# A transformer block on one core: attention scores on two row tiles and single-column sums on four column tiles

## The reference

```
mod = silu(c) @ ada_w + ada_b                  # 6 x 1024 shifts, scales and gates, one vector
h = rmsnorm(x, norm1_w) * (1 + scale1) + shift1
... = split(h @ w_in)                          # linear attention, 3 x 4 heads of dilated attention, merge gates
# dilated attention: group g of (window, dilation) = (128, 1), (512, 4), (2048, 16), 4 heads of width 64
s = einsum('brhnid,brhnjd->brhnij', q, k) / 8, masked to the band
m = max(s); p = exp(s - m); o = p @ v / sum(p)
o = sum over the groups, weighted by softmax(lse)
x = x + gate1 * (mixed @ w_out)
h2 = rmsnorm(x, norm2_w) * (1 + scale2) + shift2
x = x + gate2 * (ffn(h2) @ w_down)
return rmsnorm(x, final_norm_w)
```

## Time and profile before

| | |
|---|---|
| median of 3 runs | 909.78 us |
| the profiled execution | 910.8 us |
| its span | 909.0 us |
| granted clock over the span | 0.994 |
| TensorE busy | 890.8 us (98%) |
| VectorE, ScalarE busy | 494.3 us (54%), 368.8 us (41%) |
| TensorE waits, all: line 1780, first transfer | 7.0 us |
| line 2250 for ScalarE | 1.3 us |
| line 1817 and 1829 for VectorE | 1.0 and 0.4 us |
| line 1928 for ScalarE | 0.4 us |
| line 2282 for VectorE | 0.2 us |

### The profile page before, as it was taken

The page is one execution under the profiler, slowest core; times in us unless marked ns, Lnnn a source line. Parts: engine busy times, 40 slices in busy tenths (PEclk is TensorE's granted clock), DMA queues, the critical chain, the costliest instruction groups (busy, mean ns, idle before and its releaser), DMA issues.

```text
span 909.0 us, 12266 instructions
## 1 busy us (share of the span) xinstructions
PE 890.8 (98%) x4859; PEld 759.7 (84%) x4859; DVE 494.3 (54%) x580; ACT 368.8 (41%) x461; POOL 35.9 (4%) x33
## 2 busy tenths in 40 slices
PE   6999999999999999999999999999999999999996
PEld 5998888989898988888888888888888888888885
DVE  6877875637372757432544576555555556433333
ACT  6542216594544464531224344333333333322225
POOL 0010000000000000000022200000000000000003
PEclk9999999999999999999999999999999999999998
DMA  9985735214351534542324331333333332322202
GB/s 326 290 258 162 196 88 154 58 53 139 140 186 47 186 110 169 185 139 93 139 93 139 93 93 55 102 107 104 95 92 92 92 92 92 137 94 92 93 1 92
DMA packets 117135, 112.94 MB, mean 124 GB/s; under 512 B 7412, under 2 KB 107126, under 8 KB 114663
## 3 DMA queue, kind: packets, MB, share of 16 engines
q1 hardware_dynamic: 116375, 110.21, 38.9%
q10 hardware_dynamic: 720, 2.16, 0.7%
HBM read 104.80 MB, written 4.21 MB: 120 GB/s over the span
## 4 chain that ended last, share of the span: by engine, by line
PE 91%; SPq 2%; DMA 2%; DVE 2%; issue 1%; ACT 1%; DVEq 0%; ACTq 0%
PE bank L1773 26%; PE bank L1775 26%; PE bank L1774 26%; DMA ada_in<-in_ada_w_dram 1%; PE bank L2282 1%; SPq L446 1%; PE bank L2119 1%; PE bank L1917 1%; PE bank L1955 1%; PE bank L2047 1%; DVE ada_in L1155 1%; PE bank L1912 1%; PE bank L1889 1%; PE bank L2124 1%; SPq L510 1%
## 5 line engine op out<-in xcount | busy, mean ns | idle before, releaser
L1773 PE MATMUL bank<-h_hi,w_hi 128*128 128x512 f32 x672 | 264.7, 394 | 0.0
L1775 PE MATMUL bank<-h_hi,w_lo 128*128 128x512 f32 x672 | 261.7, 389 | 0.0
L1774 PE MATMUL bank<-h_lo,w_hi 128*128 128x512 f32 x672 | 261.6, 389 | 0.0
L1775 PEld LDWEIGHTS bank<-h_hi,w_lo 128*128 128x128 f32 x672 | 126.1, 188 | 26.6
L1773 PEld LDWEIGHTS bank<-h_hi,w_hi 128*128 128x128 f32 x672 | 126.2, 188 | 25.9 <-issue 0.2
L1774 PEld LDWEIGHTS bank<-h_lo,w_hi 128*128 128x128 f32 x672 | 126.2, 188 | 25.4 <-issue 0.2
L1228 DVE TENSOR_TENSOR w_lo<-raw,w_hi 128x2048 fp32r<-128x2048 f32 (+2 forms) x44 | 81.1, 1854 | 87.5 <-ACT w_hi L673 87.4
L1235 DVE TENSOR_TENSOR w_lo<-raw,w_hi 128x2048 fp32r<-128x2048 f32 x31 | 71.1, 2292 | 86.3 <-ACT w_hi L681 86.3
L1727 DVE SCALAR_TENSOR_TENSOR conv<-bank,vecs,conv 128x511 f32<-128x511 f32 x88 | 65.7, 748 | 65.8 <-ACT conv L1087 60.3
L673 ACT ACTIVATE w_hi<-raw 128x2048 fp32r<-128x2048 f32 (+2 forms) x42 | 67.9, 1631 | 48.2 <-DMA raw<-in_w_in_dram 35.4
L681 ACT ACTIVATE w_hi<-raw 128x2048 fp32r<-128x2048 f32 x31 | 59.1, 1905 | 69.3 <-PE bank L1775 69.3
(11 more groups left out here) (282 smaller groups left out, 1249.5 us busy)
## 6 DMA issues: line engine op xcount, KB each, us to landing
raw<-in_w_up_dram SPq DMA_DIRECT2D x44, 512.0 KB, 4.6
raw<-in_w_in_dram SPq DMA_DIRECT2D x17, 1024.0 KB, 5.3
raw<-in_ada_w_dram SPq DMA_DIRECT2D x16, 1024.0 KB, 5.5
raw<-in_w_in_dram SPq DMA_DIRECT2D x22, 512.0 KB, 5.4
raw<-in_w_down_dram SPq DMA_DIRECT2D x22, 512.0 KB, 3.7
ada_in<-in_ada_w_dram SPq DMA_DIRECT2D x16, 512.0 KB, 9.3
raw<-in_w_gla_branch_dram SPq DMA_DIRECT2D x4, 1024.0 KB, 5.0
raw<-in_w_out_dram SPq DMA_DIRECT2D x4, 1024.0 KB, 5.8
```

The costliest lines, as they stand in the source:

```text
L1773: pe.matmul(out_ap, wh, xh, start=first, stop=False, skip_group_check=True)
L1774: pe.matmul(out_ap, wh, xl, start=False, stop=False, skip_group_check=True)
L1775: return pe.matmul(out_ap, wl, xh, start=False, stop=last, skip_group_check=True)
```

## The change

It has four parts. (1) Every single-column sum is made by `column_sum` as four matmuls, each with 32 of the 128 columns of weights, on the four column tiles. (2) The sums of a later third of the modulation are one block ahead of the product (`ada_block`). (3) `qk` puts head 0 of a pair on partitions 0 to 63 and head 1 on 64 to 127, and the scores of both heads are issued in turn, into two banks. Banks 0 and 1 of the scores are made in step 0, banks 2 and 3 in step 1, for both heads; before, the first step held the first head (but for the first pair's bank 3), the second step the second head. Banks 2 and 3 wait for the masks of banks 0 and 1, whose places in PSUM they take. (4) On VectorE a step has all four masks ahead of its maxima, and the rotation of the next tile stands ahead of `attention(0, 1)` instead of behind it.

```diff
-            ("qk", 0, [DH, GROUPS, 2, 2, SEQ], F32), ("rope", 24, [P, 2, 2, SEQ], F32),
+            ("qk", 0, [P, GROUPS, 2, SEQ], F32), ("rope", 24, [P, 2, 2, SEQ], F32),
...
+        def score_bank(bk, hd):
+
+            return side[bk % 2 * 2 + hd]
...
                 for half in range(2):
                     for a in range(4):
-                        sp.dma_start(qk[32 * half:32 * half + 32, g, a // 2, a % 2, :],
+                        at = a % 2 * DH + 32 * half
+                        sp.dma_start(qk[at:at + 32, g, a // 2, :],
                                      rope[32 * a:32 * a + 32, j % 2, half, :]).then_inc(qk_in[j % 2], 16)
...
-                if (p, i) == (0, 0):
-                    mask_and_max(0, range(3))
-                elif i in (0, 1):
-                    if (p, i) == (0, 1):
-                        mask_and_max(0, range(3, 4))
-                    mask_and_max(2 * p + i)
+                if i in (0, 1):
+                    for bk in (2 * i, 2 * i + 1):
+                        masks(p, bk)
+                    for bk in (2 * i, 2 * i + 1):
+                        maxima(p, bk)
...
                     elif g == 1:
                         split_lo(n + 1)
+                        rotate(GROUPS + g, 0)
                         attention(0, 1)
-                        rotate(GROUPS + g, 0)
...
+            def column_sum(dst, at, weights, moving, first, last):
+
+                for c in range(4):
+                    part = slice(32 * c, 32 * (c + 1))
+                    done = pe.matmul(dst[part, at:at + 1], weights[:, part], moving, start=first, stop=last,
+                                     skip_group_check=True)
+                return done
...
+            def ada_block(r):
+
+                dst = take(TILE[("ada", r)])
+                pe.wait_ge(raw_used, RAW_AT[("ada", KT * (r + 1) - 1)] + 1)
+                for j in range(2 * KT):
+                    last = column_sum(dst, j, ada_acc[:, j * P:(j + 1) * P], ones[:, 0:1], j == 0, True)
+                last.then_inc(acc_ready, 1)
+
+            def scores(p, bk):
...
+                if p > 0 and bk == 0:
+                    pe.wait_ge(pt_act, 4 * p)
+                    pe.wait_ge(pt_dve, 4 * p)
+                if bk >= 2:
+                    pe.wait_ge(msk_done, 8 * p + 2 * (bk - 2) + 2)
...
+                for n, (col, queries, keys) in enumerate(parts):
+                    for hd in range(2):
+                        rows = slice(hd * DH, (hd + 1) * DH)
+                        last = pe.matmul(score_bank(bk, hd)[:, col:col + keys.stop - keys.start], qk[rows, g, 0, queries],
+                                         qk[rows, g, 1, keys], start=True, stop=True, skip_group_check=True)
+                        if n == len(parts) - 1:
+                            last.then_inc(sc_done, 1)
```

More of the change, by code:

```diff
@@ L1302, in rotate, with masks @@
                     dve.tensor_tensor(rope[:, j % 2, :, :], rope[:, j % 2, :, :], rope_t[:, :, :], ALU.add).then_inc(rope_sum, 1)
-            def mask_and_max(hh, banks=range(4)):
-                p, hd = divmod(hh, 2)
+            def masks(p, bk):
                 prev_own, own = cst[:, C_MSK:C_MSK + 2 * P], cst[:, C_MSK + P:C_MSK + 2 * P]
@@ L1310, in mask_and_max @@
                 two = prev_own.rearrange("p (a n) -> p a n", a=1).broadcast_to((P, 2, 2 * P))
[L1311 to L1316, removed]
+                at, w = BANK_AT[bk], BANK_W[bk]
+                for hd in range(2):
+                    dve.wait_ge(sc_done, 8 * p + 2 * bk + hd + 1)
+                    if p > 0:
+                        dve.wait_ge(tr_ps, 8 * (p - 1) + 4 * hd + bk + 1)
+                    dst, src = S[:, hd, at:at + w], score_bank(bk, hd)[:, 0:w]
                     if bk == 1:
@@ L1323, in mask_and_max, with maxima @@
                     dve.tensor_tensor(dst, src, m, ALU.add).then_inc(msk_done, 1)
-                for bk in banks:
-                    dve.wait_ge(msk_done, 4 * hh + bk + 1)
-                    at = BANK_AT[bk]
+            def maxima(p, bk):
+                at = BANK_AT[bk]
+                for hd in range(2):
+                    dve.wait_ge(msk_done, 8 * p + 2 * bk + hd + 1)
                     if hd == 0 and bk == 0 and p > 0:
@@ L1816, in shift_scale @@
                     for n in range(4):
-                        last = pe.matmul(bank[7][:, 4 * j + n:4 * j + n + 1], ada_rows(j, rows)[:, n * P:(n + 1) * P],
-                                         moving[:, rows:rows + 1], start=(n == 0 and (first or j not in DIRECT)),
-                                         stop=not first, skip_group_check=True)
+                        last = column_sum(bank[7], 4 * j + n, ada_rows(j, rows)[:, n * P:(n + 1) * P],
+                                          moving[:, rows:rows + 1], n == 0 and (first or j not in DIRECT), not first)
                 last.then_inc(mod1_ps, 1)
@@ L1828, in first_shift_scale @@
                 for n in (kk, kk + 2):
[L1829 to L1830 removed]
+                    last = column_sum(bank[7], n, ada_rows(0, 0)[:, n * P:(n + 1) * P], ones[:, 0:1], n == 0, True)
                 last.then_inc(first_ps if kk == 0 else mod1_ps, 1)
@@ L1843, in product @@
                 i = TILE[(UNITS[n], t)]
[L1844 to L1848, removed]
+                if (UNITS[n], t) in WITH_ADA:
+                    ada_block(WITH_ADA[UNITS[n], t])
                 dst = take(i)
@@ L1894, in scores @@
-            def scores(hh, banks=range(4)):
-                p, hd = divmod(hh, 2)
-                if hh == 0:
+            def ada_block(r):
[5 more added lines that the diff above has]
+            def scores(p, bk):
+                if p == 0 and bk == 0:
@@ L1897, in scores @@
                     pe.wait_ge(vw_act, NB)
                     pe.wait_ge(vw_dve, NB)
[L1899 to L1909, removed]
-                            lo = max(b - 1, 0) * P
-                            keys = slice(lo, (b + 1) * P)
-                            last = pe.matmul(side[bk][:, col:col + (b + 1) * P - lo], qk[:, 0, 0, hd, b * P:(b + 1) * P],
-                                             qk[:, 0, 1, hd, keys], start=True, stop=True, skip_group_check=True)
-                    else:
-                        for r in range(DIL):
-                            tok = slice(r * P, (r + 1) * P)
-                            last = pe.matmul(side[bk][:, r * P:(r + 1) * P], qk[:, bk - 1, 0, hd, tok],
-                                             qk[:, bk - 1, 1, hd, tok], start=True, stop=True, skip_group_check=True)
-                    last.then_inc(sc_done, 1)
@@ L1959, in attention @@
             def attention(p, i):
-                if (p, i) == (0, 0):
-                    scores(0, range(3))
-                elif (p, i) == (0, 1):
-                    scores(0, range(3, 4))
-                    scores(1)
-                elif i in (0, 1):
-                    scores(2 * p + i)
+                if i in (0, 1):
+                    for bk in (2 * i, 2 * i + 1):
+                        scores(p, bk)
                 if i == 4:
```

38 lines of the change are left out of this document (18 added, 20 removed).

## The result

The changed kernel takes 897.76 us (median of four runs, 897.37 to 898.01), the kernel before beside it 909.76 us; the ratio is 0.9866 [0.9849, 0.9883]. The gain is 12.0 us where 10.6 were forecast: 899.2 us was predicted. The direction and the likeliest case are right. Two terms of the sum are too small: the modulation blocks (3.4 us forecast, 4.4 measured) and the first pair (1.6 forecast, 2.8 measured).

What follows compares the result with a forecast made beforehand. TensorE, busy 98% of the span, was taken to bound the kernel. Savings of 3.4 + 1.5 + 0.9 + 1.6 + 3.2 = 10.6 us gave 899.2 us on the median's scale, range 897.7 to 903.0.

Steps and rivals of the forecast that it cites:

- the likeliest case: Whole kernel: all terms come as forecast, 899.2 us on the median's scale; chance 0.52.
- the modulation blocks: Sums in two modulation blocks on four column tiles, in one run: each block 3.58 to 1.87 us, saving 3.4 us together.
- the first pair: Scores at 107 to 120 us: TensorE gains 3.3 us but keeps 1.6, since VectorE's maxima then decide the exchange.
- 60 cycles: Skill's cost per matmul, against the column-tiled sums: if each record paid 25 ns, all 60 sums would bring under 2 us.
- First 55 us: Twenty early single-column sums on column tiles: TensorE and VectorE move forward together by 1.5 us, at least 0.4.
- End: Two groups of sums at the program's end, on the chain; the second waits for ScalarE's square: 0.9 us saved.
- Overlap of row tiles: Scores of two heads on two row tiles run together: a pair of heads takes 3.8 us instead of 7.0.
- loads in turn: Rival for scores: only weight loads take turns, 128-column scores gain nothing, 901.2 us; 0.19 together with no overlap.
- Emptying on a change of tile: Rival for scores: changing row tile waits until the array empties, 15.1 us more on scores, 919.1 us; chance 0.03.
- Second pair: Scores at 156 to 169 us on two row tiles: TensorE saves 3.2 us; q_in's evacuation keeps its size.
- Clock: Rival: granted clock falls to 1.2 GHz at transpose gaps or modulation blocks, costing 1.7 us a fall, 900.9; chance 0.25.

Runs made afterwards that it cites:

- e5: The changed kernel with each modulation block's matmuls ordered one column tile after the other, same records: 907.18 us, ratio 0.996.
- p1: The changed kernel with the column-tiled modulation sums in five pieces between the product's k steps instead of one run: 900.48 us, ratio 0.9893.
- e6: The changed kernel with 16 moving columns instead of one for each sum in the modulation blocks: 897.98 us, ratio 0.9865.
- e7: The changed kernel with 32 moving columns instead of one for each sum in the modulation blocks: 897.82 us, ratio 0.9861.
- p2: The changed kernel with every sum one plain matmul again, the modulation sums in five pieces between the product's k steps: 904.27 us, ratio 0.9938.
- e1: The changed kernel with every sum one plain matmul again, the modulation sums still in one run: 907.71 us, ratio 0.997.
- p4: The kernel before with only the column-tiled sums, modulation sums in one run; scores, masks and maxima as before: 903.71 us, ratio 0.9928.
- e4: The changed kernel with both heads' queries and keys on partitions 0 to 63, all scores on one row tile: 902.94 us, ratio 0.9921.
- r1: The changed kernel measured again, nothing altered: 898.0 us, ratio 0.9863.
- e3: The changed kernel with VectorE's rotation of the next tile moved back behind the first head's maxima: 898.48 us, ratio 0.9867.
- e2: The changed kernel with all matmuls of head 0, then all of head 1, inside a bank instead of alternating: 899.5 us, ratio 0.9882.

## Why the prediction was right or wrong, point by point

**Single-column sums, modulation blocks: the failed step.** "48 matmuls of one head in 1.32 us, 27.5 ns each ... A sum then costs 4 x 27.5 = 110 ns, my value." That divides a run by all its matmuls as if every tile had an equal share. It doesn't: in `within` 4 of the 12 matmuls of a block go to column tile 0 and only 2 to tile 3. The trace of before shows the period, in rows I hadn't used (TensorE's timeline, the same kind of record in three successive blocks):

```profile
221.06 0.22 PE L2011 MATMUL bank<-q_in,k_in 128*32 128x16 f32 x3
...
221.36 0.23 PE L2011 MATMUL bank<-q_in,k_in 128*32 128x16 f32 x4
...
221.66 0.23 PE L2011 MATMUL bank<-q_in,k_in 128*32 128x16 f32 x4
```

One block every 0.30 us, and 8 records on its busiest tile: 37 ns a record. A sum has 2 records on each of four tiles that work together: 2 x 37 = 74 ns, not 110. A block is then 16 x 74 = 1.18 us, which is what the trace has, plus 0.20 for the change back where I took 0.11. It saved 2.2 us, not 1.7; both blocks 4.4 to 4.5, not 3.4. e5 shows that the tiles work beside each other: one after the other the same records take 3.84 us at full clock. It doesn't show the 37: a tile that works alone takes 30 ns a record, four in turn take 37 each, or 34 by the slope of p1's pieces, which leaves out the way in. What makes the difference between 30 and 34 is open. e6 and e7 show that the columns played no part.

Of the Trainium skill's 60 cycles, 25 ns, for each matmul (TensorEngine Tiling, Instruction Overhead) I had said that it fits only if a float32 matmul counts once. It doesn't fit then either: 1.18 us for 64 matmuls is 18 ns each, 9 ns a record.

**First 55 us: right, as far as it can be told.** Forecast 1.5, 1.9 in the two profiles. The profiled execution of before had the granted clock at 0.50 from 32 to 35 us; p2, with the same plain sums, had 1.00 there and reached its first scores 0.5 us before it:

```profile
106.91 1.79 PE L1931 MATMUL bank<-qk 64*128 64x256 f32 x16
```
But one pair of executions is too few for this term. The first scores start at 105.4 to 106.4 us in the eleven profiles with tiled sums, and at 106.4, 106.9 and 107.4 in the three with plain ones (e1, p2, before): the means are 1.0 us apart. The medians give 1.3 (6.4 of p4, less 4.4 for the blocks and 0.7 for the end). The profile of the changed kernel is an early one and that of before the latest, which accounts for 0.9 of the 1.2 us by which the two differ more than the medians.

**End: right.** 0.9 forecast, 0.7 to 0.8 found; both groups of sums take 0.43 + 0.43 us, and the second waits for ScalarE's square, as said. One wait was not in the forecast: the transposes behind the sums now wait 0.32 us for ScalarE's x, so the sums are no longer on the chain there.

**Overlap of row tiles: right.** 3.8 us forecast for a pair, 1.79 + 2.06 = 3.85 measured; e4 shows it to be the row tiles' own doing. Of the rivals, loads in turn would have left the 128-column scores as they were, and they halve. Emptying on a change of tile falls with them. The Trainium skill's rule (TensorE: Matmul & The Clock Gate, The mechanism) that loads of another row group overlap a running matmul agrees with this: 32 records of 128 columns take 2.06 us, and 3.84 on one row tile.

**Second pair: right.** 3.2 forecast, 3.3 in the profile. ScalarE's exponentials still came behind other work, and q_in's evacuation kept its 0.60 us.

**First pair: right in mechanism, too small; the second failed term.** The chain is as drawn: shuffles first, then the maxima as the last releaser of the exchange, TensorE waiting for S. It gave 2.8 instead of 1.6. The forecast lets TensorE stand still for "some 2 us ahead of and between the transposes"; the profile has 0.21 + 0.52 where 0.40 stood, because S comes earlier than forecast. Worked along the chain against the earlier trace rows: the exchange goes out 3.83 us earlier, 1.92 of it from the first 55 us, so 1.9 from the maxima where I had 1.6. Behind it I had left everything as it was, and another 0.9 came there: SyncE's first issue takes 0.37 instead of 0.58, the first transfer 3.97 instead of 4.04, the second 1.91 instead of 2.50. The two transfers in the chain of before:

```profile
126.89 4.04 DMA mx_dram<-mx
...
131.35 2.50 DMA mx_other<-mx_dram
```

This is not the luck of one execution. From the first scores of the first pair to those of the second, the kernel before has 49.0 us:

```profile
107.39 1.78 PE L1912 MATMUL bank<-qk 64*128 64x256 f32 x8
...
156.40 1.78 PE L1912 MATMUL bank<-qk 64*128 64x256 f32 x8
```

p4, the other profile in the old order, has 49.2. The eight profiles whose scores and steps are those of the changed kernel (after, r1, e1, e5, e6, e7, p1, p2) have 45.7 to 46.4, though their second transfer is anything from 1.74 to 2.73 us. From SyncE's issue of the exchange to the exponentials these eight have 7.1 to 7.8 us, and before, p4 and e4, with one row tile, 8.0 to 8.5; why is not shown. e4 has 48.4 between the same scores, so the order alone is worth 0.6 to 0.7 us in this stretch, which agrees with the 0.8 between its median and that of p4.

**Clock: the rival didn't come about, but it is real.** The changed kernel has 1.00 in its blocks and between its transposes, where two gaps of 0.21 and 0.52 us came instead of the four of up to 0.9 that the rival had. The same sums cost 3.4 us more where the clock fell (e1 against p2).

## What to carry to other kernels

Price a run of tiled matmuls by the records of its busiest tile, not by their number: 34 to 37 ns here for 32 columns of weights on four tiles in turn (30 on one tile alone), with 1 to 32 columns streamed alike, and about 0.3 us to go in and out of it. Before dividing a run's time by its count, look at which tiles it uses. And where a chain leaves one releaser for another, follow it to the end in the rows; and read a term of one or two microseconds from several executions, not from one pair of profiles.

## What the runs showed of the hardware that was not expected

- A run of single-column records alone pulled the granted clock down to 1.2 GHz though TensorE counted as busy throughout: plain (e1) and one tile after the other (e5). In the first block of each it fell before the run was over (4.52 and 4.59 us), in the second 0.3 to 0.5 us behind it (3.47 and 3.84 us). Runs of 1.18 us, and pieces of up to 1.01 us between product steps (p2), kept 2.4 GHz. The Trainium skill (TensorE: Matmul & The Clock Gate, HAM oscillation) lays such a fall to idle gaps of the engine; here there was none.
- After a wait of 1.85 us (e3) the clock was 0.50 for 2 us; after 0.52 us (the changed kernel) it stayed at 1.00.
- Changing between plain and column-tiled records costs time on both sides: about 0.1 us going in, 0.20 coming out before a 128x512 product (p1).
- Column tiles work beside each other: 128 single-column records with 32 columns of weights take 1.18 us on four tiles in turn and 3.84 us tile after tile, both at 1.00 (e5).
- Two row tiles overlap even when the heads don't alternate strictly (e2): 1.89 and 2.82 us where no overlap has 3.30 and 3.84.
